# A fused ten-stage transformer kernel: fewer loads of ScalarE's table before the reciprocal square roots

## The reference

```python
def rmsnorm(x, g):
    xf = x.astype(jnp.float32)
    y = xf * lax.rsqrt(jnp.mean(xf * xf, axis=-1, keepdims=True) + NORM_EPS)
    return (y * g.astype(jnp.float32)).astype(x.dtype)

def macaron_layer(x, mixer, ...):
    x = x + FFN_HALF * rmsnorm(swiglu(rmsnorm(x, ffn1_pre_g), ...), ffn1_post_g)
    x = x + rmsnorm(mixer(rmsnorm(x, mix_pre_g)), mix_post_g)
    x = x + FFN_HALF * rmsnorm(swiglu(rmsnorm(x, ffn2_pre_g), ...), ffn2_post_g)
    return x
```

```python
x = layer_norm(DN_ALPHA * x + g1 * y, ln1_g[l], ln1_b[l])
```

## Time and profile before

| what | value |
|---|---|
| median of three runs | 3681.71 us (3674.12 to 3683.87) |
| the profiled execution, its own time | 3680.46 us |
| its span, first to last instruction | 3678.7 us |
| TensorE busy (matmuls) | 3462.1 us, 94% |
| VectorE, ScalarE busy | 1940.8 us, 1354.4 us |
| mean granted clock of TensorE | 0.966 of full |
| table loads of line 1370 | 42, 53.9 us |

### The profile page before, as it was taken

The page is one execution under the profiler, slowest core; times in us unless marked ns, Lnnn a source line. Parts: engine busy times, 40 slices in busy tenths (PEclk is TensorE's granted clock), DMA queues, the critical chain, the costliest instruction groups (busy, mean ns, idle before and its releaser), DMA issues.

```text
span 3678.7 us, 47128 instructions
## 1 busy us (share of the span) xinstructions
PE 3462.1 (94%) x20308; PEld 2757.2 (75%) x20308; DVE 1940.8 (53%) x2721; ACT 1354.4 (37%) x1977; POOL 4.4 (0%) x18
## 2 busy tenths in 40 slices
PE   8999896889999999989999999989999999889998
PEld 6888675778888788867578887766788877568886
DVE  5554566356543654343445434566666355656654
ACT  4322454133322432233533322244444233544433
POOL 0000000000000000000000000000000000000000
PEclk9999996799999999999999999999999999999999
DMA  5444330024444342222012223310232231012221
GB/s 183 138 148 139 118 106 19 3 69 137 139 148 138 124 133 98 98 77 75 1 58 98 97 96 110 105 52 24 80 104 97 98 131 58 24 52 98 93 103 58
DMA packets 93087, 342.41 MB, mean 93 GB/s; under 512 B 10320, under 2 KB 10960, under 8 KB 92368
## 3 DMA queue, kind: packets, MB, share of 16 engines
q1 hardware_dynamic: 92880, 339.40, 27.3%
HBM read 337.26 MB, written 2.10 MB: 92 GB/s over the span
## 4 chain that ended last, share of the span: by engine, by line
PE 85%; DVE 7%; ACT 6%; issue 1%; DMA 0%; SPq 0%; ACTq 0%; DVEq 0%
PE ps L754 20%; PE ps L755 20%; PE ps L756 20%; PE ps L771 3%; PE ps L772 3%; PE ps L775 3%; PE ps L794 1%; PE ps L795 1%; PE ps L796 1%; ACT SPH L1366 1%; ACT WK L1802 1%; DVE SPL L1894 1%; PE ps L1136 1%; ACT L1370 1%; PE ps L1126 1%
## 5 line engine op out<-in xcount | busy, mean ns | idle before, releaser
L1894 DVE TENSOR_TENSOR SPL<-RAW,SPH 128x1024 fp32r<-128x1024 f32 x522 | 636.8, 1224 | 1094.8 <-ACT SPH L1366 1094.6
L754 PE MATMUL ps<-HH,SPH 128*128 128x512 f32 x2352 | 932.5, 396 | 23.6 <-DVE WK L2237 8.1
L1366 ACT ACTIVATE SPH<-RAW 128x1024 fp32r<-128x1024 f32 x522 | 548.3, 1055 | 1085.2 <-PE ps L756 967.1
L755 PE MATMUL ps<-HL,SPH 128*128 128x512 f32 x2352 | 920.9, 392 | 0.0
L756 PE MATMUL ps<-HH,SPL 128*128 128x512 f32 x2352 | 920.4, 391 | 0.0
L754 PEld LDWEIGHTS ps<-HH,SPH 128*128 128x128 f32 x2352 | 445.1, 189 | 130.7 <-issue 10.2
L755 PEld LDWEIGHTS ps<-HL,SPH 128*128 128x128 f32 x2352 | 445.0, 189 | 95.6 <-issue 4.4
L756 PEld LDWEIGHTS ps<-HH,SPL 128*128 128x128 f32 x2352 | 444.7, 189 | 93.8
L754 PE MATMUL ps<-AH,SPH 128*128 128x512 f32 x1152 | 449.6, 390 | 0.0
L756 PE MATMUL ps<-AH,SPL 128*128 128x512 f32 x1152 | 448.3, 389 | 0.0
L755 PE MATMUL ps<-AL,SPH 128*128 128x512 f32 x1056 | 410.8, 389 | 0.0
(11 more groups left out here) (430 smaller groups left out, 3619.6 us busy)
## 6 DMA issues: line engine op xcount, KB each, us to landing
RAW<-in_ws SPq DMA_DIRECT2D x522, 512.0 KB, 3.3
RAW<-in_wa SPq DMA_DIRECT2D x96, 512.0 KB, 3.3
WK<-in_sm SPq DMA_DIRECT2D x2, 2784.0 KB, 10.5
WK<-in_cst SPq DMA_DIRECT2D x2, 1664.0 KB, 7.0
X<-in_x SPq DMA_DIRECT2D x8, 256.0 KB, 7.8
out<-X SPq DMA_DIRECT2D x8, 256.0 KB, 2.1
WK<-in_sm SPq DMA_DIRECT2D x1, 768.0 KB, 5.3
PCT<-in_pc SPq DMA_DIRECT2D x1, 349.0 KB, 3.0
```

What stands on the lines that cost most here:

```text
L754: e.matmul(out, wh, rhs[0], start=start, stop=False)
L755: e.matmul(out, wh, rhs[1], start=False, stop=False)
L1366: e.activation(SPH[:, q:q + 1024], RAW[:, r:r + 1024], ACT.Copy).then_inc(hi_ready.did(("hi", n)))
L1894: e.tensor_tensor(SPL[:, q:q + 1024], RAW[:, r:r + 1024], SPH[:, q:q + 1024].bitcast(F32), ALU.subtract).then_inc(lo_ready.did(("lo", n)))
```

## The change

`rsqrt_of` takes an argument that says whether it loads the table. It still does for the first reciprocal square root of FFN1 (`s == 0`), for that of the recurrence's chunk 0 (`c == 0`), and for the four of the retention branch (line 1768, not in the diff). It no longer does for the input norms of the five other stages, for `rcol`, for the six `rsqrt_of_y`, for the four `layer_norm`, and for chunks 1 to 3. The loads at m == 7 and all others stay.

```diff
-            def rsqrt_of(src, out, eps, scale, first, second):
-                ln_exp_table()
+            def rsqrt_of(src, out, eps, scale, first, second, load=True):
+
+                if load:
+                    ln_exp_table()
...
-                rsqrt_of(ps["xsum", s][:], RS[:], EPS6, 1.0, ("xln", s), ("rs", s))
+                rsqrt_of(ps["xsum", s][:], RS[:], EPS6, 1.0, ("xln", s), ("rs", s), s == 0)
...
-                rsqrt_of(ps["ysum", s][:], RS[:], EPS6, 1.0, ("yln", s), ("yrs", s))
+                rsqrt_of(ps["ysum", s][:], RS[:], EPS6, 1.0, ("yln", s), ("yrs", s), False)
...
-                        rsqrt_of(ps["fvar", c][:], scr["fq", c], EPSG, 1.0 / 64, ("fln", c), ("frs", c))
+                        rsqrt_of(ps["fvar", c][:], scr["fq", c], EPSG, 1.0 / 64, ("fln", c), ("frs", c), c == 0)
...
-                rsqrt_of(ps["rcolp",][:, 0:4], rcol, EPS6, 1.0, ("rcln",), ("rcol",))
+                rsqrt_of(ps["rcolp",][:, 0:4], rcol, EPS6, 1.0, ("rcln",), ("rcol",), False)
...
-                rsqrt_of(RS[:], RS[:], EPS5, 1.0, ("yln", s), ("yrs", s))
+                rsqrt_of(RS[:], RS[:], EPS5, 1.0, ("yln", s), ("yrs", s), False)
```

## The result

| | kernel before | changed kernel |
|---|---|---|
| median of 6 runs | 3679.66 us (3674.12 to 3684.2) | 3652.39 us (3647.52 to 3656.51) |
| ratio, 95% interval | | 0.9923 (0.9911 to 0.9936) |
| span of the profiled execution | 3678.7 us | 3651.5 us |
| table loads of line 1370 | 42 | 23 |

The change is 27.3 us faster, 0.7%. The forecast was 3661.0 us, 20.7 us faster, so 6.6 us less than came. With the interval, the gain is 23.5 to 32.7 us.

The account below looks back on a forecast made before the run. TensorE, busy 94% of the span, bounds the kernel, so ScalarE loads pay only where TensorE waits. Stage ends 7.8 + 5.2 plus input norms 7.7 make 20.7 us: 3681.7 - 20.7 = 3661.0 us, range 3651 to 3669.

Parts of the forecast that it names:

- Which loads go: Line 1370, on ScalarE: 19 of 42 table loads go, 23 stay, nothing is added or moved.
- price of one: End of FFN1: the load stands wholly behind the wait, so Ln can start 1.30 us earlier without it.
- Ends of stages: Boundaries between stages: six loads behind RMS norms give 7.8 us, four in layer norms 5.2 us.
- VectorE's margin of 0.24 us: Layer norms at stage ends: VectorE idles 1.54 us and loses 1.30, leaving 0.24 us to spare.
- Input norms: MIX0, FFN2, FFN3, FFN4 and two loads in MIX1: TensorE's waits shrink, 7.7 us in all.
- Chunks 1 to 3: Three loads costed at nothing, hidden behind TensorE's work or early results; 3.9 us if the cover were gone.
- No other wait longer by more than some tenths: Profile of the changed kernel: no TensorE wait besides the named ones should grow by more than some tenths.
- The clock, taken at nothing: TensorE's half-clock stretches after boundary waits: same stretches, a little shorter on average, nothing taken for them.
- the nine starts: Nine 8 us stretches from a stage's first projection: granted clock 0.67 to 0.80, losing 19.0 us, expected to stay there.
- The clock that stays up: Rival: clock stays up after the shorter boundary waits, up to 19.0 us more, 3642 us; chance 0.05.
- both rivals: Compiler puts loads back: two per place, 3702.5 us, chance 0.03; or one per place, 3682 us, chance 0.03.
- The absorbed gain: Rival: input norms' gain lost as weight chunks arrive no earlier, only stage ends count, 3668.7 us; chance 0.06.

Follow-up runs that it names:

- the run with both loads: Kernel before with a load of another set (exp) put ahead of each of the 19 loads: 3709.15 us, 31.8 over the kernel before.
- the ends alone: Kernel before with only the ten loads at the ends of stages taken out: 3667.88 us, 16.2 under the kernel before.
- the experiment on input norms alone: Kernel before with only the six input-norm loads of MIX0, FFN2, FFN3, FFN4 and MIX1 taken out: 3676.03 us, 8.0 under it.
- The second set of runs: The unaltered changed kernel timed again beside new runs of the kernel before: 3655.47 us, 23.1 under it (17.7 to 27.6).
- the first group: Experiments timed together on one chip beside the kernel before, whose median there was 3684.0 us.
- filler: Changed kernel with 6 or 8 small matmuls of constants while TensorE waits at each later stage's start: 3638.46 us, 17.0 under the changed kernel.

## Why the prediction was right, and where it fell short

**Which loads go; price of one.** Right: 19 went, 23 are left, and Ln starts 1.30 us earlier. The drain that the Trainium skill gives for a switch (ScalarE: Activation LUTs, "What ACT_TABLE_LOAD costs") was weighed and set aside; the 38 switches of the run with both loads show none either: the next instruction started 1.29 or 1.30 us after each load did. Here the measurement differs from the page, and the measurement decides.

**Ends of stages, 7.8 and 5.2 us.** Right by the waits, each one, and VectorE's margin of 0.24 us was 0.26. By the times, the ends alone gave 16.2 us (12.5 to 22).

**Input norms, 7.7 us.** Right: the waits are within 0.1 us of what was written, FFN4's is gone, and the experiment gave 8.0.

**Chunks 1 to 3, nothing.** Right: with the three loads back, TensorE's idle time in MIX0 is the same 70.4 us. The times alone couldn't have told 3.9 us.

**No other wait longer by more than some tenths.** Wrong: that for the key norms grew by 2.0 us, and line 964 stood 2.9 us longer, part of it scatter. Other waits took back 2.3 of the 20.6 us.

**The clock, taken at nothing.** If a term of the sum was mis-sized, it is this one. For the nine starts it was right (19.0 us to 17.8). What it left out was the time at half clock inside the stages, above all in MIX0 and HYB1, where TensorE's idle time is 70 and 26 us. In the profiled pair the matmuls took 8.9 us less, in other pairs as little as 1.4; 3.2 of them are in HYB1 and 4.3 in MIX0 (353.5 to 349.2 us of TensorE's busy time). HYB1's share has the same sign in two profiles each of the kernel before and of the changed kernel, but it isn't what a saved load is worth: HYB1 was also shorter with loads added (319.7 us). MIX0's share can't be told from scatter: its length was 419.6 and 426.8 us in the changed kernel's own two profiles, and 424.6 and 423.8 in the kernel before's. HYB1 alone gave 3.4 and 7.4 us beyond its load in the two profiles. The second set of runs, however, was only 2.4 us over the forecast, and its interval takes the forecast in. So how much of the first set's 6.6 us is a real excess stays open.

**The range: its reason right, its lower end partly luck.** The time came out at 3652.4 us, 1.4 above the lower end of 3651. That end was made of a gain from the chunks and of all nine starts at 0.80, and neither came; 2.0 of the 8.6 us below the forecast are the kernel before itself, whose median was 3681.7 over three runs and 3679.7 over six.

I wrote that the clock is a large part of why runs differ. The 21 runs of the kernel before in the first group bear it out: the shortest, 3670.76 us, had a mean granted clock of 0.969, the longest, 3688.06 us, one of 0.964. 0.005 of the span is 18.4 us, and they are 17.3 apart.

**The rivals.** The clock that stays up is refuted for waits of 3.7 us; it takes filler to bring it about, and it is then worth 17 us by the times, near the 17.8 that the nine stretches lose in the changed kernel. No load was put in by the compiler, neither one nor two: both rivals fall by the row of 23 and by ScalarE's count of instructions, 1958 in place of 1977. The absorbed gain falls by the experiment on input norms alone.

Not settled: what decides which gaps inside MIX0 and HYB1 end in half clock. In most stages the pattern repeats from run to run in one program and differs a little between programs; in HYB1 it repeated in the kernel before, and differed by 4.0 us between two executions of the changed kernel. One profile per edit can't separate what the edit did from that, and no run here was made to.

## What to carry to other kernels

In these runs a table load cost its full length, 1.30 us, where it stood between a wait and an activation that TensorE needed, and nothing where TensorE had other work meanwhile. So count loads behind waits, leave out those whose set is active, and move the others ahead of the wait. In a kernel that is bound by TensorE with short idle gaps, split a difference into waits and busy time of the same matmuls: the second scattered here by 3 to 4 us between executions of one program, more than twice a load. Take two profiles of each program before a few microseconds of it are put down to an edit. Where TensorE must idle for some microseconds ahead of dense work, filler matmuls into a free bank were worth more here (17 us) than the whole of the input norms' loads (8 us).

## What the runs showed of the hardware that was not expected

- The half-clock time of a program repeats from run to run in most stages, not in all. Two profiles of the kernel before agreed within 0.1 us in each of eight stages of 315 to 384 us, though one reached them 2.4 us earlier. Two of the changed kernel agreed within 0.1 us in six of these stages and differed by 4.0 us in HYB1. MIX0, with 70 us of idle time, differed by 0.8 and 7.2 us.
- A load of the set that is already active takes 1283 ns all the same: all 42 of line 1370 did, and 19 of them could go without another load appearing. One right behind a load of the same set doesn't reach the chip.
- Two loads of different sets in a row took 1.28 and 1.30 us; nothing like a drain was seen between them or before the next activation, at 19 places.
- Matmuls of 384 columns whose results are thrown away held the granted clock at 1.00 over waits of 3.7 and 4.7 us, where behind idle waits of that length it was 0.66 to 0.81 over 8 us, nine of nine.
